# Last FFN of a two-layer fp32 trunk: separate places for the weights' sums and low parts, three pairs of banks for the downs, and POOL's subtractions in halves

## The reference, cut to what matters

```python
def rmsnorm(x, g):
    xf = x.astype(jnp.float32)
    y = xf * lax.rsqrt(jnp.mean(xf * xf, axis=-1, keepdims=True) + EPS)
    return (y * g).astype(x.dtype)

def swiglu(h, w_up, w_down):
    g, u = jnp.split(h @ w_up, 2, axis=-1)
    return (jax.nn.silu(g) * u) @ w_down

# per layer: x = x + mixer(rmsnorm(x, norm_mix[layer]), ...)
#            x = x + swiglu(rmsnorm(x, norm_ffn[layer]), ffn_w_up[layer], ffn_w_down[layer])
```

## Time and profile before

| | us |
|---|---|
| runs shown: median of 3 (lowest to highest) | 2499.15 (2495.69 to 4963.62) |
| profiled execution, its own time | 2495.07 |
| span of the profile, first to last instruction | 2493.1 |
| PE busy | 2412.8 |
| DVE, POOL, ACT busy | 1200.8, 1071.3, 910.4 |
| mean granted clock of TensorE | 0.991 |

### The profile page before, as it was taken

One profiled execution on the slowest core, in us unless ns is written; L12 is line 12 of the kernel. 1 busy time (PEld: TensorE's weight loads), 2 busy tenths in 40 slices (PEclk: granted clock), 3 DMA queues, 4 the chain that ended last, 5 costly groups with the idle time before them and its releaser, 6 DMA issues.

```text
span 2493.1 us, 37403 instructions
## 1 busy us (share of the span) xinstructions
PE 2412.8 (97%) x15246; PEld 2165.7 (87%) x15246; DVE 1200.8 (48%) x1987; ACT 910.4 (37%) x1222; POOL 1071.3 (43%) x627
## 2 busy tenths in 40 slices
PE   8999999899999999999999999999999998999998
PEld 6889987688887977999999889988887897899988
DVE  3513245334445445443344433344433439877776
ACT  5331135233223355443333343244432223433433
POOL 2722145555455344545345450053445434444443
PEclk9999999999999999999999999999999999999999
DMA  8863363321323477422223274422242432222222
GB/s 309 304 217 136 138 252 117 115 77 60 123 80 123 164 265 267 144 68 94 85 77 102 68 279 171 162 87 85 77 131 85 159 134 89 85 102 85 99 97 77
DMA packets 102249, 335.90 MB, mean 135 GB/s; under 512 B 12288, under 2 KB 16192, under 8 KB 102080
## 3 DMA queue, kind: packets, MB, share of 16 engines
q1 hardware_dynamic: 102080, 333.52, 38.8%
HBM read 255.20 MB, written 76.16 MB: 133 GB/s over the span
## 4 chain that ended last, share of the span: by engine, by line
PE 81%; DVE 8%; issue 2%; DVEq 2%; POOL 2%; POOLq 1%; ACT 1%; DMA 1%; SPq 0%; ACTq 0%
PE ps L965 52%; PE ps L1054 17%; PE ps L1023 6%; POOL wl L1663 1%; POOLq L1668 1%; DMA wr<-in_wblk 1%; DVE wql L1916 1%; PE ps L1093 1%; PE ps L1149 1%; PE ps L1147 1%; DVEq L1905 1%; DVE hf L1944 0%; PE ps L989 0%; DVE wqr L1903 0%; DVE sq L1855 0%
## 5 line engine op out<-in xcount | busy, mean ns | idle before, releaser
L1663 POOL TENSOR_TENSOR wl<-wr,wh 128x1024 fp32r<-128x1024 f32 (+1 forms) x262 | 635.6, 2437 | 518.0 <-ACT wh L1355 517.6
L965 PE MATMUL ps<-xh,wh 128*128 128x260 f32 (+3 forms) x2592 | 740.5, 333 | 6.3 <-issue 2.2
L965 PE MATMUL ps<-xl,wh 128*128 128x260 f32 (+3 forms) x2592 | 727.2, 328 | 0.0
L965 PE MATMUL ps<-xh,wl 128*128 128x260 f32 (+1 forms) x2576 | 725.2, 329 | 0.0
L965 PEld LDWEIGHTS ps<-xh,wh 128*128 128x128 f32 (+1 forms) x2592 | 435.5, 187 | 61.2 <-issue 17.9
L965 PEld LDWEIGHTS ps<-xl,wh 128*128 128x128 f32 (+1 forms) x2592 | 435.1, 187 | 44.7 <-issue 2.4
L965 PEld LDWEIGHTS ps<-xh,wl 128*128 128x128 f32 x2576 | 433.0, 188 | 44.8
L1355 ACT ACTIVATE wh<-wr 128x1024 fp32r<-128x1024 f32 (+2 forms) x266 | 274.2, 1042 | 236.2 <-DMA wr<-in_wblk 227.9
L1054 PE MATMUL ps<-hidh,wh 128*128 128x512 f32 (+1 forms) x704 | 215.5, 347 | 25.3 <-POOL wl L1663 11.0
L1054 PE MATMUL ps<-hidl,wh 128*128 128x512 f32 (+1 forms) x704 | 211.9, 341 | 0.0
L1054 PE MATMUL ps<-hidh,wl 128*128 128x512 f32 (+1 forms) x704 | 211.3, 341 | 0.0
(11 more groups left out here) (416 smaller groups left out, 3587.4 us busy)
## 6 DMA issues: line engine op xcount, KB each, us to landing
wr<-in_wblk SPq DMA_DIRECT2D x262, 512.0 KB, 3.6
split<-wh SPq DMA_DIRECT2D x64, 512.0 KB, 5.3
split<-wl SPq DMA_DIRECT2D x64, 512.0 KB, 6.2
wh<-split SPq DMA_DIRECT2D x64, 512.0 KB, 3.2
wl<-split SPq DMA_DIRECT2D x64, 512.0 KB, 4.2
wqr<-in_wblk SPq DMA_DIRECT2D x44, 512.0 KB, 4.2
dwr<-in_wblk SPq DMA_DIRECT2D x22, 512.0 KB, 4.3
xr<-in_xT SPq DMA_DIRECT2D x8, 260.0 KB, 6.1
```

Source lines behind the costliest of these rows:

```text
L965: mm = pe.matmul(ps[0:cols, b + c, 0:n], wt[:, w], xt[:, e:e + n], start=first, stop=end)
L1663: pool.tensor_tensor(lo, raw, hi.bitcast(F32), ALU.subtract).then_inc(s_lo, 1)
```

## The change

- Sums: `set_sums(f, n)` makes one of the four sums, each at a place of its own; `sums_lo(f, n)` makes the low part of one sum (512 columns) instead of two (1024). The lists `sums`, `lows` and `highs` give the places for each set; sets 1, 2 and 3 have their own. Odd sets from 5 on have two of their low parts behind (f, 1), in their own slice.
- The multiplication of hf by the gate, until now in the evacuation of product 6, is an item of its own (`sm2`): behind all else of (f, 6) in slices without downs behind them, and behind down 0 in those with downs. hidh follows it, or down 1; hidl of odd slices goes from behind down 1 to behind down 3.
- Banks: the downs of this FFN take pairs 0, 2, 6 in turn over all eighty of them and leave the turn of the products as it is. The norm of part A, in banks 6 and 7, waits for the evacuations that stand before it.
- Sums of squares, norm and `fin` of part A are placed anew (squares at slices 4 to 11 instead of 4 to 14, the norm at (14, 1) instead of (16, 0), `fin` in slices 16, 18, 20, 21 instead of 17 to 20).
- In the run into the last FFN, `xn`, `xt`, `xh` come earlier; xl 0 and 1 stand ahead of the last downs but one; low parts of set 0 are four pieces.
- POOL's `weights_lo` makes each block's low part in two halves of 512 columns, for all blocks in the kernel but the small ones.

```diff
@@ -124,13 +124,19 @@
                     add(("wq", f + 2))
                 for s in at.get((f, i), ()):
                     add(s)
-            add(("hh", 1, B, g, kk))
             if f + 2 == NF:
                 add(("wd", NG - 1))
-            if kk and g:
+            if not (kk and g):
+                add(("sm2", f))
+                add(("hh", 1, B, g, kk))
+            else:
                 for m in range(KT):
                     add(("down", 1, B, g - 1, m))
+                    if m == 0:
+                        add(("sm2", f))
                     if m == 1:
+                        add(("hh", 1, B, g, 1))
+                    if m == 3:
                         add(("hl", 1, B, g, 1))
                     for s in at.get((f, "down", m), ()):
                         add(s)
@@ -297,45 +303,56 @@
...
-    at = {(0, i): [(s, 1, j)] for i, s, j in ((0, "wH", 1), (2, "wH", 2), (4, "wH", 3), (3, "wL", 2), (5, "wL", 3))}
+                           (9, "down", 5): [("wS", 0, n) for n in range(4)], (9, "down", 6): [("xn", 0)],
+                           (9, "down", 7): [("xn", 1), ("xn", 2)],
+                           (10, 0): [("xn", 3), ("xh", 0), ("xn", 4), ("xn", 5), ("xn", 6)],
+                           (10, 1): [("xn", 7), ("xh", 1), ("xh", 5), ("xt", 0)], (10, 2): [("xt", 1), ("xh", 4), ("xt", 2)],
+                           (10, 3): [("xl", 0), ("xl", 1), ("xh", 3), ("xh", 2)],
+                           (10, "down", 0): [("wH", 0, 0), ("xh", 6)], (10, "down", 1): [("xl", 2)],
+                           (10, "down", 2): [("wH", 0, 1)], (10, "down", 3): [("xl", 3)], (10, "down", 4): [("wH", 0, 2)],
+                           (10, "down", 5): [("xl", 4)], (10, "down", 6): [("wH", 0, 3)],
+                           (10, "down", 7): [("wq", 1), ("xl", 5)], (NG, "down", 0): [("wL", 0, 0)], (NG, "down", 1): [("wL", 0, 1)],
+                           (NG, "down", 2): [("wL", 0, 2)], (NG, "down", 3): [("wL", 0, 3)],
+                           (NG, "down", 4): [("xl", 6)], (NG, "down", 6): [("wS", 1, 0)],
+                           (NG, "down", 7): [("wS", 1, 1), ("wH", 1, 0), ("wd", 0)]}))
+    at = {}
...
-            places = ((1, 2), (1, 3), (1, 4), (1, 5), (2, 0))
+        at.setdefault((f, step) if isinstance(step, int) else (f, *step), []).extend(x)
...
+    def downs(m):
+        return ("down", m)
...
+    for f in range(1, NF):
+        if f == 1:
+            sums, lows, highs = (None, None, (0, 1), (0, 1)), ((0, 4), (0, 5), (0, 6), (1, 1)), (None, (0, 0), (0, 2), (0, 3))
+        elif f == 2:
+            sums, lows = ((1, 1), (1, 3), (1, 4), (1, 5)), ((1, 6), (2, 1), (2, 1), (2, 3))
+            highs = ((1, 3), (1, 4), (1, 5), (1, 6))
...
-            places = ((2, 2), (2, 3), (2, 4), (2, 5), (2, 6))
+            sums, lows = ((2, 3), (2, 4), (2, 5), (2, 6)), ((3, 1), (3, 1), (3, 3), (3, 4))
+            highs = ((2, 4), (2, 5), (2, 6), (2, 6))
...
-            places = ((f - 2, "down", 6), (f - 1, 0), (f - 1, 1), (f - 1, 2), (f - 1, 4))
+            sums = ((f - 2, downs(2)), (f - 2, downs(3)), (f - 1, 1), (f - 1, 1))
+            lows, highs = ((f - 1, 5), (f - 1, 6), (f, 1), (f, 1)), ((f - 1, 1), (f - 1, 2), (f - 1, 3), (f - 1, 4))
...
-            places = ((f - 1, 3), (f - 1, 4), (f - 1, 5), (f - 1, "down", 1), (f - 1, "down", 4))
-        for n, p in enumerate(places):
-            put(p[0], p[1:], ("wH", f, n - 1) if n else ("wS", f))
...
-        put(places[4][0], places[4][1:], ("wL", f, 2))
-        last = (2, 1) if f == 2 else (3, 0) if f == 3 else (f - 1, 5) if f % 2 else (f - 1, "down", 6)
...
+            sums, lows = ((f - 1, 3), (f - 1, 4), (f - 1, 5), (f - 1, downs(1))), tuple((f - 1, downs(m)) for m in (4, 5, 6, 7))
+            highs = tuple((f - 1, downs(m)) for m in (1, 2, 2, 4))
+        for kind, places in (("wS", sums), ("wH", highs), ("wL", lows)):
+            for n, p in enumerate(places):
+                if p:
+                    put(*p, (kind, f, n))
...
+        put(*first, ("wD", g, 0))
+        put(*second, ("wD", g, 1))
...
-        put(4 + m + m // 2, (2,), ("xs", 8, m))
-    put(16, (0,), ("nrm", 8), ("nrv", 8))
...
-        put(17 + m // 2, (1,), ("fin", m))
...
-        put(17 + m // 2, (6,), ("fo", m))
+        put(4 + m, 2, ("xs", 8, m))
+    put(14, 1, ("nrm", 8), ("nrv", 8))
+    for m, f in enumerate((16, 18, 20, 21)):
+        put(f, 3, ("fin", 2 * m))
+        put(f, 4, ("fin", 2 * m + 1), ("fo", 2 * m))
...
@@ -359,6 +378,8 @@
...
+            if k == "nrm":
+                self.at_norm[x[1]] = count["D"]
...
@@ -370,6 +391,11 @@
             if nb == 2 and cur % 2:
                 cur += 1
             b = cur % 4
+            if k == "down" and x[1:3] == (1, B):
+
+                b = (0, 2, 6)[n_downs % 3]
+                n_downs += 1
+                cur -= nb
             if k == "sp" and x[2] in (2, 4):
 
                 b = 4 + x[2] // 4
@@ -1007,10 +1033,10 @@
             def product(u, f, i):
 
                 pe.wait_ge(s_qhi, 4 * f + PSTEP[i] + 1)
-                if PSTEP[i] < 2:
+                if i < 3:
                     pe.wait_ge(s_qlo, 2 * f + PSTEP[i] + 1)
                 else:
-                    pe.wait_ge(s_qld, 2 * f + PSTEP[i] - 1)
+                    pe.wait_ge(s_qld, 4 * f + i - 2)
                 if f == 0:
                     pe.wait_ge(s_xh, KT * 7 + XQ[i] + 1)
                     pe.wait_ge(s_xl, KT * 7 + i + 1)
@@ -1100,6 +1126,8 @@
...
+                if n == 8:
+                    pe.wait_ge(s_evd, pl.at_norm[n])
...
@@ -1660,7 +1688,11 @@
                 raw, hi, lo = wr[n % 4][:, 0:w], wh[n % 4][:, 0:w], wl[n % 4][:, 0:w]
                 if w == KT * 16:
                     raw, hi, lo = side_by_side(n % 4)
-                pool.tensor_tensor(lo, raw, hi.bitcast(F32), ALU.subtract).then_inc(s_lo, 1)
+                    pool.tensor_tensor(lo, raw, hi.bitcast(F32), ALU.subtract).then_inc(s_lo, 1)
+                    return
+                for e in (slice(0, w // 2), slice(w // 2, w)):
+                    last = pool.tensor_tensor(lo[:, e], raw[:, e], hi[:, e].bitcast(F32), ALU.subtract)
+                last.then_inc(s_lo, 1)
 
             def x_squares(n, m):
                 X = NORMS[n][0]
@@ -1895,24 +1927,24 @@
                 v.wait_ge(s_xh, KT * 7 + XQ[i] + 1)
                 v.tensor_tensor(xql[i][:], xqr[i], xqh[i][:].bitcast(F32), ALU.subtract).then_inc(s_xl, 1)
...
-            def set_sums(f):
...
-                a11, a12, a21, a22, s2, s1, s4, s3 = (wqr[f % 2][:, 512 * n:512 * n + 512] for n in range(8))
+            def set_sums(f, n):
...
+                a11, a12, a21, a22, s2, s1, s4, s3 = (wqr[f % 2][:, 512 * i:512 * i + 512] for i in range(8))
                 v.drain()
-                v.wait_ge(s_wq[f % 2], 32 * (f // 2 + 1))
-                v.tensor_tensor(s1, a21, a22, ALU.add)
-                v.tensor_tensor(s3, a11, a21, ALU.subtract)
+                if n == 0:
+                    v.wait_ge(s_wq[f % 2], 32 * (f // 2 + 1))
+                    v.tensor_tensor(s1, a21, a22, ALU.add)
+                elif n == 1:
+                    v.tensor_tensor(s3, a11, a21, ALU.subtract)
+                elif n == 2:
+                    v.tensor_tensor(s2, s1, a11, ALU.subtract)
+                else:
+                    v.tensor_tensor(s4, a12, s2, ALU.subtract).then_inc(s_wsum, 1)
...
+            def sums_lo(f, n):
                 v.drain()
-                v.tensor_tensor(s2, s1, a11, ALU.subtract)
-                v.drain()
-                v.tensor_tensor(s4, a12, s2, ALU.subtract).then_inc(s_wsum, 1)
...
-            def sums_lo(f, j):
-                if j < 2:
-                    return
-                v.drain()
-                v.wait_ge(s_qhi, 4 * f + j + 1)
-                e = slice(512 * PAIRS[j][0], 512 * PAIRS[j][1])
+                v.wait_ge(s_qhi, 4 * f + 3 + n // 2)
+                e = slice(512 * (4 + n), 512 * (5 + n))
                 v.tensor_tensor(wql[f % 2][:, e], wqr[f % 2][:, e], wqh[f % 2][:, e].bitcast(F32), ALU.subtract).then_inc(s_qld, 1)
...
             def products_sum(it, f, i):
@@ -1939,9 +1971,12 @@
                     v.drain()
                     v.tensor_tensor(hf[:, t + Q:t + 2 * Q], part(4), usum[:], ALU.add).then_inc(s_evd, 1)
                     v.tensor_tensor(hf[:, t:t + Q], usum[:], part(2), ALU.subtract).then_inc(s_evd, 1)
-                    v.drain()
-                    v.wait_ge(s_gsi, f + 1)
-                    v.tensor_tensor(hf[:, t:t + 2 * Q], hf[:, t:t + 2 * Q], gsum[:], ALU.mult).then_inc(s_hm, 1)
+
+            def gate_times_value(f):
+                t = (2 * (f // 2 % 2) + f % 2) * W[B]
+                v.drain()
+                v.wait_ge(s_gsi, f + 1)
+                v.tensor_tensor(hf[:, t:t + 2 * Q], hf[:, t:t + 2 * Q], gsum[:], ALU.mult).then_inc(s_hm, 1)
 
             def weights_lo(n):
                 w = block_cols(n)
@@ -2464,11 +2499,13 @@
...
-                    set_sums(z[0])
```

(3 more changed lines are left out.)

14 lines of the change are left out of this document (3 added, 11 removed), and 6 rows, old and new, of the table outs.

## The result

| us | before | after | predicted |
|---|---|---|---|
| median (lowest to highest) | 2497.89 (2495.69 to 4963.62, 4 runs) | 2538.39 (2533.65 to 2543.91, 4 runs) | 2520 (2477 to 2538) |
| ratio | 1 | 1.0166 [1.0137, 1.0195] | 1.008 |
| profiled execution | 2495.07 | 2536.3 | 2520 |
| its span | 2493.1 | 2534.5 | |
| start of the last FFN at | 2096.5 | 2092.6 | 7 earlier |

The changed kernel is slower by 1.66%, 40 us. That is clear of the noise (the interval of the ratio lies wholly above 1), though less than 2%, and 0.4 us above the upper end of the forecast's range. One of the four runs of the kernel before took 4963.62 us, twice the others; the ratio leaves it out. Of the 41.2 us between the two profiled executions the first four slices hold 15.0 (predicted 10), the nine rounds 30.1 (20) and the run-in -3.9 (-7).

The account below looks back on a forecast made before the run. PE, busy 2412.8 of 2493.1 us, was taken as the bound, waiting for DVE, which POOL holds up. Terms +20 + 10 - 3 + 1 - 4 = +24 to +25 on 2495.07 gave 2520 us, range 2477 to 2538.

Parts of the forecast that it names:

- first four slices: Start of the last FFN, four slices with their downs: waits before slices 2 and 3, 67.3 us against 57.1, +10.
- nine rounds: Rounds behind the first four slices, each an even slice, an odd slice and eight downs: 334 us against 314.1, +20.
- run-in: Stretch into the last FFN: -3 us there, and -4 from POOL's halves elsewhere.
- What bounds the kernel: Whole kernel: PE is busy 2412.8 of 2493.1 us, so only moments in which PE waits can be won.
- T0: Moment in a round when the odd slice starts on PE; the forecast's times in the round count from it.
- late pair: Bank pair of products 5 and 6; a first down on it waits from T0+11.5 to T0+14.2.
- the next slice's bank: First bank of the next slice, last used by down 5, 6 or 7; 7 costs 1.0 us at least.
- the wait of down 7: Last down of a round: waits 1.0 us for accumulation 4, which ends at T0+23.9.
- rival C: Rounds: the clock follows the waits, 3.2 us lost in each of nine, 29 more, 2549 us; chance 0.07.
- the wait ahead of the half downs: End of the last FFN: the half downs start behind a down 7, +1 us.
- A: Last FFN: DVE keeps pace, its operations rarely meet POOL's, rounds of 32.9 us, 2480 us; chance 0.26.
- B: Last FFN: even, half of the collisions, two waits won and two new, say 2498 us; chance 0.15.

Follow-up runs that it names:

- after, memset: Kernel after, with POOL setting the down weights' low parts in the last FFN to zero by memset instead of computing them; 2501.42 us, 1.0014.
- after, four edits: Kernel after with sums of sets 2 and 3 early, odd sets' low parts in the even slice, gate multiplication ahead, three bank pairs in fixed order; 2511.99 us.
- before with what gained: Kernel before with POOL halves, three bank pairs in fixed order, squares, norm and fin as in after, sums of sets 2 and 3 earlier; 2473.23 us.
- before_halves: Kernel before with POOL's block subtractions in halves, nothing else; 2491.02 us, 0.9978.
- the kernel with the old pairs: Kernel after with the downs' banks back in the old turn of two pairs; 2530.52 us, 1.013.

## Why the prediction was wrong in size and right in kind

The step that failed is the size of two terms of the sum, and most of all the clock in them. The nine rounds were given nothing for a lower clock and lost 4.7 us by it; the first four slices were given 1.6 and lost 6.5. That is 9.6 of the 16.3 us between 2520 and the profiled 2536.3. Some 4 us more are DVE's lateness in the odd slice and behind it, and 3 us a gain of the run-in and the halves that did not come. These errors all point one way. The median passes the upper end of the range by only 0.4 us, but its centre was off by 16.

The trace of the kernel before already had what was missing. The sum counted all waits of a regular round (2.5 us together, clock at 1.00) and took from it that such waits leave the clock alone. But the two rounds at 0.91 and 0.95 each have one wait of 2.5 and 2.7 us in a piece, before down 1, and the clock fell at it both times (mean 0.54 over the 7.4 us from 2384.5, 0.50 over the 3.4 from 2422.6). The forecast itself put single waits of 2.7 and 2.8 into the rounds.

Groups of DVE in the first eight rounds of the kernel after, each operation on two SBUF tensors (count, busy us, mean ns):
```profile
L1948 DVE TENSOR_TENSOR wql<-wqr,wqh 128x512 fp32r<-128x512 f32 x64 | 65.7, 1026 | 6.2 <-issue 0.4
...
L1936 DVE TENSOR_TENSOR wqr<-wqr 128x512 f32<-128x512 f32 x16 | 18.5, 1154 | 1.5
...
L1979 DVE TENSOR_TENSOR hf<-hf,gsum 128x520 f32<-128x520 f32 x16 | 17.6, 1101 | 1.5
```
The same groups across the kernels (those of the other two sums, L1940 and L1942, with them), in us:

| first eight rounds | low parts | four sums | gate | together | all nine rounds |
|---|---|---|---|---|---|
| before | 43.2 (33 x 1.31) | 57.6 | 13.9 | 114.7 | 314.3 |
| after | 65.7 (64 x 1.03) | 59.1 | 17.6 | 142.4 | 344.4 |
| after, memset | 45.9 (63 x 0.73) | 59.2 | 11.2 | 116.3 | 313.7 |
| after, four edits | 52.8 (65 x 0.81) | 65.9 | 18.0 | 136.7 | 327.5 |
| before with what gained | 43.1 (33 x 1.31) | 56.9 | 12.1 | 112.1 | 298.8 |

A low part of 1024 columns took 1.31, 0.08 over its time alone; a piece of 512 took 1.03, 0.34 over it. A hold comes once for each operation, and there are twice as many of them, standing where POOL works. How much is the number and how much the place was not separated: no run splits the low parts at the old places. The kernel with four edits says that the place weighs much, since its 65 pieces took 0.81 each, 0.12 over the time alone. hidl, not in the table, has two SBUF inputs too and grew from 11.0 to 15.0.

*What bounds the kernel* held: PE's moments of waiting for DVE, with POOL behind DVE. Every place that the text named shows in the trace: the waits before products 5 and 6 of the odd slice (1.4 and 0.17 in the mean; predicted 1.15 and 0.25), its end at T0+11.5 to 12.1 (11.5), the late pair at downs 0, 1 and 2 in the order written out, the next slice's bank (2.7 us in rounds 3 and 4, 1.3 in rounds 5 and 6), the wait of down 7 (0.6 to 1.1, and 2.4 with down 6's in the two rounds with the late pair at down 2; 1.0).

*Nine rounds, +30 for +20.* The 10.5 us between 344.4 and 334 lie in four places. The clock: rounds 2, 4 and 5 had 0.96, so 0.04 x (38.8 + 40.8 + 38.6) / 0.5 = 9.5 us at 1.2 GHz, 4.7 lost; the sum gave the rounds nothing for it and left it all to rival C. The odd slice and its last usum: the waits before product 5 came to 12.7 for 9 x 1.15 = 10.4, and usum ended at T0+14.3 to 15.0 instead of 14.2, 0.5 in the mean; with both, some 4 together are left beyond the clock and what was set aside for the squares and the norm. The last of the nine was put at 34.8 although the list has its late pair first, which by the text's own T0+14.2 makes 35.8: a slip of 1.0. And the wait ahead of the half downs, 0.9, falls into this round as these stages are cut; the prediction had it as +1 of its own.

*Start of the last FFN, +15 for +10.* Again the clock, mostly: 0.09 x 71.9 / 0.5 = 12.9 us at 1.2 GHz, 6.5 lost, where the step took 3.5 us and 1.6: +4.9. (By the same working 7 us at 1.2 GHz lose 3.5, not the 3.2 of the text, and half of it is 1.8.) It took one wait for the cause, as long as 5.9, and half a disturbed round for the price; slice 2 with the wait behind it ran at 0.89, and slice 3 with its downs at 0.84. The wait before slice 3 was 6.0 (5.9). The one before slice 2 was 3.9 instead of 2.8, since its last sum ended 1.2 behind the slice's end and not with it. Slice 3 did not run as the others: PE waited 2.1 us before its product 3, for a low part on DVE held beside POOL's down blocks, which no term had (with the memset it is 0.5). Even so the rest is 1.4 under the 26.8 taken for slice 3 and its downs.

*Run-in and halves, -3.9 for -7.* before_halves alone gives -5; moving the other items of the run-in gave nothing beyond the variation of that start. The halves cost POOL 62 us, not 44 (1.36 each, not 1.27 to 1.30). PE's waits for POOL's wl grew from 11.0 us to 14.9, where the text had +1, and to 15.0 in before_halves; shorter waits for DVE made up for that.

*Rivals.* A (DVE keeps pace) fell: the usum waits grew. B fell with it. C was right in kind at a sixth of its price in the rounds: three drops in nine rounds, 4.7 us against its 29, and more time at the lower clock in the first four slices. The forecast should have held that middle: the waits before slices 2 and 3 and both of 2.7 us were followed by a lower clock, one of two waits of 3.3 was, neither of those of 2.9, and none of 1.9 or less in the rounds of the kernel with the old pairs.
